# Two projections wait for pairs of feature blocks, retention scores stand beside value tiles, one read-out changes banks, and one stick-breaking step changes its order

## What is computed

```python
# block 1: the attention branch's projection and the cross attention's output projection
merged = sigmoid(g_ssd) * (y_ssd @ w_proj_ssd) + sigmoid(g_att) * (y_att @ w_proj_att)   # "pa"
o = einsum('bhtm,bmhd->bthd', p, v).reshape(b, s, 1024)
mem_out = o @ w_mo                                                                       # "mo"
# block 2, retention: 4 heads, q and k 256 wide after the rotation, v 512 wide
scores = einsum('bhnd,bhmd->bhnm', q, k) * decay                                         # "rs"
o = einsum('bhnm,bhme->bhne', scores, v)                                                 # "on"
o = normalise(o)
out = (silu(g) * o).reshape(b, s, 2048) @ w_out                                          # "rg", "ro"
# block 2, stick-breaking: 16 heads of 64
z = q @ k.T / 8
log_keep = where(causal, log_sigmoid(-z), 0)
between = reverse_cumsum(log_keep) - log_keep                                            # the "sums"
w = where(causal, exp(log_sigmoid(z) + between), 0)
out = (w @ v) @ w_out                                                                    # "values", "so"
```

## Time and profile before

| | |
|---|---|
| median of 3 runs | 2739.38 us (2735.33 to 2743.34) |
| the profiled execution's own time | 2731.21 us |
| its span | 2729.1 us |
| mean granted TensorE clock | 0.982 |
| TensorE busy | 2617.5 us, 96% |
| VectorE, ScalarE busy | 1931.0 us (71%), 1535.5 us (56%) |
| DMA | 632.28 MB, mean 232 GB/s |
| TensorE in the chain that ended last | 86% |

### The profile page before, as it was taken

The page is one execution under the profiler, slowest core; times in us unless marked ns, Lnnn a source line. Parts: engine busy times, 40 slices in busy tenths (PEclk is TensorE's granted clock), DMA queues, the critical chain, the costliest instruction groups (busy, mean ns, idle before and its releaser), DMA issues.

```text
span 2729.1 us, 34419 instructions
## 1 busy us (share of the span) xinstructions
PE 2617.5 (96%) x14799; PEld 2263.3 (83%) x14799; DVE 1931.0 (71%) x1924; ACT 1535.5 (56%) x1618; POOL 50.7 (2%) x38
## 2 busy tenths in 40 slices
PE   8998999998999999999979999999999999989998
PEld 7998887797998977998967888888888888867877
DVE  4557688565556665545668898898989898976864
ACT  4446565343444343444647777677777777755753
POOL 0000000000001000001000000000000000010000
PEclk9999999998999999999979999999999999999999
DMA  6545343452555534585338999999999999965432
GB/s 252 186 164 198 135 148 117 168 194 100 185 187 206 192 129 168 187 222 194 107 116 347 347 357 346 337 361 341 359 346 357 345 360 344 358 269 180 139 124 94
DMA packets 88944, 632.28 MB, mean 232 GB/s; under 512 B 9840, under 2 KB 9856, under 8 KB 13776
## 3 DMA queue, kind: packets, MB, share of 16 engines
q1 hardware_dynamic: 84800, 610.24, 60.3%
q0 software_dynamic: 3984, 19.76, 2.7%
HBM read 625.77 MB, written 4.19 MB: 231 GB/s over the span
## 4 chain that ended last, share of the span: by engine, by line
PE 86%; DVE 9%; ACT 3%; DMA 1%; issue 1%; DVEq 0%; POOL 0%; SPq 0%; ACTq 0%; POOLq 0%
PE pw L717 15%; PE pw L719 14%; PE pw L718 14%; PE py L717 12%; PE py L718 12%; PE py L719 12%; DVE lo L699 2%; ACT hi L696 1%; DMA raw<-in_wts 1%; PE pw L2507 1%; PE pw L2444 1%; PE pw L2445 1%; PE py L1177 1%; DVE X L940 1%; PE pw L873 1%
## 5 line engine op out<-in xcount | busy, mean ns | idle before, releaser
L699 DVE TENSOR_TENSOR lo<-raw,hi 128x2048 fp32r<-128x2048 f32 x406 | 925.8, 2282 | 382.4 <-ACT hi L696 382.2
L696 ACT ACTIVATE hi<-raw 128x2048 fp32r<-128x2048 f32 x414 | 785.9, 1900 | 387.7 <-PE py L719 317.7
L717 PE MATMUL pw<-XH,hi 128*128 128x256 f32 x1688 | 484.2, 287 | 14.2 <-DVE lo L699 6.1
L718 PE MATMUL pw<-XL,hi 128*128 128x256 f32 x1688 | 481.6, 285 | 0.0
L719 PE MATMUL pw<-XH,lo 128*128 128x256 f32 x1688 | 481.4, 285 | 0.0
L699 DVE TENSOR_TENSOR lo<-raw,hix 128x2048 fp32r<-128x2048 f32 x168 | 384.9, 2292 | 53.5 <-ACT hix L696 49.1
L718 PE MATMUL pw<-lo,GH 128*128 128x512 f32 x896 | 354.2, 395 | 0.0
L717 PEld LDWEIGHTS pw<-XH,hi 128*128 128x128 f32 x1688 | 327.9, 194 | 20.0 <-DVE lo L699 7.6
L696 ACT ACTIVATE hix<-raw 128x2048 fp32r<-128x2048 f32 x168 | 321.7, 1916 | 39.1 <-PE py L719 37.5
L718 PEld LDWEIGHTS pw<-XL,hi 128*128 128x128 f32 x1688 | 328.2, 194 | 1.1
L719 PEld LDWEIGHTS pw<-XH,lo 128*128 128x128 f32 x1688 | 327.9, 194 | 0.0
(11 more groups left out here) (512 smaller groups left out, 3800.2 us busy)
## 6 DMA issues: line engine op xcount, KB each, us to landing
raw<-in_wts SPq DMA_DIRECT2D x577, 1024.0 KB, 4.8
GB<-in_rows POOLq DMA_DIRECT2D x8, 1024.0 KB, 5.0
scratch_bias<-dr POOLq DMA_DIRECT2D x1, 3072.0 KB, 35.8
BI<-scratch_bias POOLq DMA_DIRECT2D x1, 2048.0 KB, 11.9
raw<-in_wts SPq DMA_DIRECT2D x3, 512.0 KB, 3.1
raw<-in_wts SPq DMA_DIRECT2D x2, 576.0 KB, 3.6
X<-in_x SPq DMA_DIRECT2D x1, 1024.0 KB, 5.2
nrow<-in_rows POOLq DMA_DIRECT2D x2, 512.0 KB, 5.5
```

What stands on the lines that cost most here:

```text
L696: L.e.activation(hi, raw, ACT.Copy).then_inc(*L.up("hi", n))
L699: L.e.tensor_tensor(lo, raw, f32(hi), ALU.subtract).then_inc(*L.up("lo", n))
L717: T_.e.matmul(o, x[0], w[0], start=first, stop=False)
L718: T_.e.matmul(o, x[0], w[1], start=False, stop=False)
```

## The change

`pair_turned(key)` is a function of `kx` that names the signal of the pair in which feature `kx` is; `pa` and `mo` are given it in place of `turned(key, 8)`. `pe_ret_scores` and `dve_ret_scores` become generators, one head to a step after an empty first step, and are woven with the six tiles of `rvb`; ScalarE has no part in them. The read-out of head 3 takes two W banks instead of two Y banks. In `pe_sb`, the sums of group 3 stand ahead of the wait for `svb` and of the values of group 2. No matmul, transfer or elementwise operation is added or removed.

```diff
+        def pair_turned(key):
+
+            return lambda kx, tt: [("ev", (key, kx // 2 * 2))]
...
         def pe_ret_scores(T_):
+
+            yield
             T_.wait_ge("rope", 14)
             for h in range(4):
                 for mt in range(2):
...
                     e.then_inc(*T_.up("rs", h, mt))
+                yield
 
         def dve_ret_scores(V):
+            yield
+            V.wait_ge("decay")
             for h in range(4):
                 for mt in range(2):
                     V.wait_ge("rs", h, mt)
...
+                yield
...
-                    b = Y.take(T_, ("on", h, tt))
+                    b = (W if h == 3 else Y).take(T_, ("on", h, tt))
...
             pe_sb_turn(T_, 1)
+            pe_sb_sums(T_, 3)
             for tt in range(2):
                 T_.wait_ge("ev", ("svb", 0, tt, 0))
             pe_sb_values(T_, 2)
-            pe_sb_sums(T_, 3)
             yield
...
-            weave(pe_tm(T_, "pa", (AH, AL), 8, D, D, [turned("o1", 8)]),
+            weave(pe_tm(T_, "pa", (AH, AL), 8, D, D, pair_turned("o1")),
...
-            run(pe_tm(T_, "mo", (BH, BL), 8, D, D, [turned("mot", 8)], True))
+            run(pe_tm(T_, "mo", (BH, BL), 8, D, D, pair_turned("mot"), True))
...
-            run(pe_tm(T_, "rvb", XP, 8, 1536, 512, x_of(3)))
-            pe_ret_scores(T_)
+            weave(pe_tm(T_, "rvb", XP, 8, 1536, 512, x_of(3)), pe_ret_scores(T_))
...
-            run(ev_tm(V, "rvb", 8, 1536, 512, by_both(cols_of(RV[:, :, 512:2048]))))
-            V.wait_ge("decay")
-            dve_ret_scores(V)
+            weave(ev_tm(V, "rvb", 8, 1536, 512, by_both(cols_of(RV[:, :, 512:2048]))), dve_ret_scores(V))
```

## The result

The changed kernel took 2721.81 us (median of 6 runs, 2719.84 to 2726.02), the kernel before beside it 2738.36 us (median of 6, 2735.33 to 2743.34): a ratio of 0.9949, 95% interval 0.9938 to 0.9960. By the ratio that is 14.0 us faster (11.0 to 17.0). I had forecast 7.9 us less, 2731.5 us, with a range down to 2725: the direction is right, the size is not, and the range missed the time by 3 us.

What follows compares the result with a forecast made beforehand. TensorE, busy 96% of the span, was taken to bound the kernel. 1.8 + 1.6 + 1.8 + 1.7 + 3.5 - 2.5 = 7.9 us off the median 2739.4 gave 2731.5 us; forecast's own range 4 to 11 us, with rivals 2725 to 2738 us.

Steps and rivals of the forecast that it cites:

- The four pauses: TensorE's waits at pa, mo, the retention scores and ro: shortening them gains 1.8, 1.8, 1.7 and 3.5 us.
- Pairs: At pa and mo, the first matmul waits for the first of four subtractions, not the last: 1.8 us gained each.
- Scores: Retention scores woven with value tiles: a 2.0 us wait goes, 0.3 us returns; net gain 1.7, bounds 0.5 and 2.0.
- the rival in which VectorE's splits are late: Value tiles: waiting for scores delays VectorE's weight splits, costing 16.8 us in all, 2748.3 us; chance 6%.
- The 0.5 us a burst behind my lower bound: Woven scores: each burst pays 0.5 us at its ends, giving the lower bound of 0.5 us gain.
- The bank: At ro, read-out 3 in W banks removes the wait for on: gain 3.5 us, bounds 3.0 and 5.1.
- The clock: Behind pa, the low clock after the pause goes: 1.6 us won, bounds 0 and 1.6.
- Rival 2: Sums 3 ahead of values 2 costs nothing and ro spares a low clock too: 12.5 us, 2726.9 us; chance 15%.
- The order: Stick-breaking stage, sums 3 ahead of values 2: a loss of 2.5 us, bounds 0.5 gain and 4.2 loss.
- The base: Whole kernel: the terms were taken off the runs' median of 2739.4 us, giving 2731.5 us.

Runs made afterwards that it cites:

- fill3: The kernel before with matmuls of constants put into its three pauses at pa, mo and ro, none removed: 2732.48 us, ratio 0.9985.
- order: The kernel before with only sums 3 put ahead of values 2: 2737.52 us, ratio 1.0002.
- no_order: The changed kernel with sums 3 put back behind values 2: 2722.47 us, ratio 0.9943 to the kernel before.
- no_order2: The changed kernel with sums 3 put back behind values 2, run again beside the changed kernel: 2723.26 us, ratio 0.9956 to the kernel before.
- look1: An unchanged copy of the kernel before, one profiled execution: 2737.36 us.

## Why the prediction was wrong, point by point

The four pauses went as foretold. The miss is in what the low clock takes under matmuls, in two steps: the term for it was read from one place of one execution, and the loss of the last edit was carried from its stage to the end. By the profiled executions the sum reads 8.8 (pauses) + 2.4 (clock behind `pa` and `ro`) + 1.0 (not assigned) - 2.1 (the stage) - 0.1 + 0.6 (the router) + 3.2 (third block) = 13.8 us, where I had 8.8 + 1.6 - 2.5 = 7.9. So the mis-sized clock term is 0.8 of the missing 5.9 us, and the largest piece, 3.2, lies in the third block, which my sum didn't have at all and whose link to the change is not shown. My terms' own upper bounds, 2.0 + 1.6 + 2.0 + 2.0 + 5.1 + 0.5 = 13.2 us, don't reach the measured 14.0 either, and the range of 4 to 11 us was narrower than they.

- **Pairs, 1.8 us each: right.** 1.79 and 1.80 us, waits of 1.29 and 0.28 us as foretold, and tiles wait for no later pair.
- **Scores, 1.7 us: right as far as it can be told**, -2.2 us (-4.7 to +0.3) alone; no wait for `ST` is left, and the rival in which VectorE's splits are late (2748.3 us) did not come. The 0.5 us a burst behind my lower bound stand in no row; in the changed kernel the first matmul behind a head's scores is followed after 0.31 us (934.03 to 934.34) at a pace of 0.23, so a return costs about 0.1.
- **The bank, 3.5 us: right.** The wait is gone and nothing takes its place. Alone it gave 4.9 us (2.5 to 7.4); the 1.1 us that `ro`'s clock loses on average would fit the rest, but the interval holds 3.5 itself.
- **The clock, 1.6 us: the term that was mis-sized.** I took it from one execution, which had one loss at `pa` and none at `ro`, and counted it once. Over six profiled executions both places lose 2.4 us on average; by `fill3` the clock at the three pauses is worth 4.1 us (1.6 to 6.8). Rival 2 named the loss at `ro` and had 15%. Its time, 2726.9 us, is the nearest of all, but in part by luck: in its stage the last edit did cost 2.1 us, and what gave that back lies elsewhere. The Trainium skill, TensorE: Matmul & The Clock Gate, Part 1, says that the same kernel differs from run to run in how many matmuls run slowly, since the gate is not in step with the kernel. The six executions agree: 0, 1.6 and 2.9 us behind the same 3.08 us of standing. Of one trace I should have asked what that place costs on average, not what it cost there.
- **The order, +2.5 us: right in its stage (+2.1), not seen in the total.** `order` alone gives +0.5 us (-1.9 to +3.0), which holds 2.1 too, but the changed kernel is also no slower than `no_order` and `no_order2`. The step that failed is the one from the stage to the end: a loss in one stage was carried to the end as if nothing behind it could change. 0.6 us come back at the router and 3.2 in the third block, on average over five executions that differ among themselves by as much; the latter is without a proven cause. In the stage itself I wrote that a longer pause should cost no less at the low clock. It cost less, 2.8 us under the matmuls against 3.4; my working, 5.85 us at half speed, had that right at 2.9, and the price was the longer wait.
- **The base.** I subtracted from a median of three, 2739.4; the 84 executions have 2736.9. That error of 2.5 us went the other way: from the better base, the forecast would have been 2729.0.

The account of the profiled executions, stretch by stretch: up to the scores of group 3, six of the kernel before (`order` among them, which is the same there) average 1359.6 us, six of the changed one (with either order behind) 1347.3: 12.2 us, of which 8.8 are the four pauses, 2.4 the clock behind `pa` and `ro`, and 1.0 is left, which no row here assigns. Behind that come the differences of the table above: -2.1 in the stage, -0.1, +0.6 at the router and +3.2 from the experts on, 13.8 us in all, against 14.0 by the ratio. Means of five to eleven executions that spread by 2 us and more make part of this agreement luck.

## What to carry to other kernels

A pause of TensorE of some 2 to 4 us costs its length plus a chance of a low clock behind it; size that chance from several profiled executions, or put matmuls of constants into the pause and time it, because one trace shows one draw. Count the low clock only from where the pause ends. In these runs shortening pauses paid more than their length, by 2.4 us on 8.8 where it could be read, and where a pause can't be shortened, matmuls that do nothing else are worth trying. A local loss or gain read from a stage should be checked at later landmarks too, since later clock losses need not stay as they were.

## What I had not expected of the hardware

- 3.52 us of standing at `ro` were followed by full pace in three executions, by 1.8 us lost in two and by 2.7 us in one, with identical instructions ahead of it. In `look1` the clock did not drop at once: the first records behind the pause are 0.40 us long, and from 1022.9 us, 1.6 us later, they are 0.63.
- Extra work made the kernel faster: 8 matmuls of constants by 4.1 us, and 40 by some 8 us beside the changed kernel.
- In the third block the clock took 5.0, 1.8 or 0 us from the same instructions, in stretches that no edit touches; beside a spread of 11.6 us between all executions of the kernel before.
